# RWKV-7 recurrence on one Trainium2 core: the three sums over a head's channels as two fp32r products instead of one fp32 product

## The reference, cut to what matters

```
kk = heads(k * k_k)
kk = kk / jnp.maximum(jnp.linalg.norm(kk, axis=-1, keepdims=True), L2_EPS)
k = k.astype(f32) * (1.0 + (a - 1.0) * k_a.astype(f32))
...
y = wkv7_scan(rh, heads(decay), kh, vh, kk, kk * ah)
y = head_group_norm(y, lnx_w.astype(f32), lnx_b.astype(f32))
bonus = (jnp.sum(rh * kh * r_k.astype(f32), axis=-1, keepdims=True) * vh)
y = (y + bonus.reshape(bsz, t, D_INNER)) * jax.nn.silu(g.astype(f32))
```

## Time and profile before

| | |
|---|---|
| Runs of the kernel (3) | 2086.11, 2092.5, 2094.26 us; median 2092.5 |
| Span of the profiled execution | 2084.5 us |
| Its own time | not shown apart from the runs; the nearest, 2086.11 us, is 1.6 us above the span |
| Busy in the span | PE 1908.8 us (92%), DVE 1257.7 (60%), ACT 910.5 (44%), POOL 90.9 (4%) |
| `lerp_phase` | 0 to 237 us |
| `rwkv_phase` | 237 to 894 us |
| `dense_phase` | 894 to 2084.5 us |
| Period of a steady step | 37.5 us (POOL's `ld`, L619, starts at 591.87, 629.36, 667.29 us) |
| The three sums in all | L874, L869 and L879, 16 products each |

### The profile page before, as it was taken

The page is one execution under the profiler, slowest core; times in us unless marked ns, Lnnn a source line. Parts: engine busy times, 40 slices in busy tenths (PEclk is TensorE's granted clock), DMA queues, the critical chain, the costliest instruction groups (busy, mean ns, idle before and its releaser), DMA issues.

```text
span 2084.5 us, 43656 instructions
## 1 busy us (share of the span) xinstructions
PE 1908.8 (92%) x18912; PEld 1476.3 (71%) x18912; DVE 1257.7 (60%) x1865; ACT 910.5 (44%) x1392; POOL 90.9 (4%) x119
## 2 busy tenths in 40 slices
PE   4999799899999998989999999999888599999997
PEld 3678566666666666668888888887655378888885
DVE  6562167677777877644455554546557568777532
ACT  5342245646646556533222222335445464444321
POOL 2000000000000000300000000000011000000000
PEclk9999899999999999999999999999998799999998
DMA  3225311011111110143322223231110032222331
GB/s 121 77 80 151 99 44 41 29 45 41 34 40 41 44 40 30 53 132 103 101 97 96 101 91 101 91 101 61 51 41 21 15 107 92 101 97 95 94 91 68
DMA packets 51452, 154.13 MB, mean 74 GB/s; under 512 B 8512, under 2 KB 11072, under 8 KB 51264
## 3 DMA queue, kind: packets, MB, share of 16 engines
q1 hardware_dynamic: 51264, 151.35, 22.5%
HBM read 145.04 MB, written 6.29 MB: 73 GB/s over the span
## 4 chain that ended last, share of the span: by engine, by line
PE 50%; DVE 4%; ACT 2%; issue 1%; POOL 0%; DMA 0%; POOLq 0%; DVEq 0%; ACTq 0%
PE bank L1579 14%; PE bank L1578 14%; PE bank L1580 14%; PE bank L1666 1%; PE bank L1667 1%; PE bank L1668 1%; PE bank L1703 0%; DVE room L2288 0%; DVE room L2255 0%; PE bank L1686 0%; PE bank L1747 0%; PE bank L1738 0%; PE bank L1649 0%; PE bank L1714 0%; PE bank L1711 0%
## 5 line engine op out<-in xcount | busy, mean ns | idle before, releaser
L1785 ACT ACTIVATE w_hi<-raw 128x1024 fp32r<-128x1024 f32 (+2 forms) x195 | 197.7, 1015 | 496.3 <-PE bank L1580 453.9
L1578 PE MATMUL bank<-h_hi,w_hi 128*128 128x512 f32 x896 | 349.8, 390 | 0.0
L1580 PE MATMUL bank<-h_hi,w_lo 128*128 128x512 f32 x896 | 348.6, 389 | 0.0
L1579 PE MATMUL bank<-h_lo,w_hi 128*128 128x512 f32 x896 | 348.6, 389 | 0.0
L151 DVE TENSOR_TENSOR w_lo<-raw,w_hi 128x1024 fp32r<-128x1024 f32 (+2 forms) x202 | 237.0, 1174 | 153.6 <-ACT w_hi L1785 153.1
L1579 PEld LDWEIGHTS bank<-h_lo,w_hi 128*128 128x128 f32 x896 | 168.2, 188 | 35.7 <-issue 0.7
L1578 PEld LDWEIGHTS bank<-h_hi,w_hi 128*128 128x128 f32 x896 | 168.2, 188 | 35.3 <-issue 0.7
L1580 PEld LDWEIGHTS bank<-h_hi,w_lo 128*128 128x128 f32 x896 | 168.2, 188 | 35.0
L738 ACT ACTIVATE swapT<-invT 64x256 f32<-64x256 f32 x192 | 79.7, 415 | 104.4 <-DVE invT L1291 53.9
L144 PE MATMUL bank<-xg_hi,g_hi 128*128 128x512 f32 x256 | 104.0, 406 | 21.2 <-DVE g_lo L151 11.8
L145 PE MATMUL bank<-xg_lo,g_hi 128*128 128x512 f32 x256 | 102.1, 399 | 0.0
(11 more groups left out here) (377 smaller groups left out, 4126.8 us busy)
## 6 DMA issues: line engine op xcount, KB each, us to landing
raw<-in_w_conv SPq DMA_DIRECT2D x64, 512.0 KB, 3.2
raw<-in_w_up SPq DMA_DIRECT2D x44, 512.0 KB, 3.2
raw<-in_w_out SPq DMA_DIRECT2D x32, 512.0 KB, 3.8
raw<-in_w_in SPq DMA_DIRECT2D x20, 512.0 KB, 3.3
g_raw<-in_w_g SPq DMA_DIRECT2D x16, 512.0 KB, 3.3
g_raw<-in_w_r SPq DMA_DIRECT2D x16, 512.0 KB, 3.8
w_k<-in_w_k SPq DMA_DIRECT2D x16, 512.0 KB, 3.4
w_v<-in_w_v SPq DMA_DIRECT2D x16, 512.0 KB, 3.8
```

The costliest lines, as they stand in the source:

```text
L1578: pe.matmul(to, whi, hi, start=begin, stop=False)
L1579: pe.matmul(to, whi, lo, start=False, stop=False)
L1580: last = pe.matmul(to, wlo, hi, start=False, stop=end)
L1785: act.activation(w_hi[:, g % RING, 0:width], raw[:, g % RAW, 0:width], ACT.Copy).then_inc(S("whi"), 1)
```

## The change

Each of the three sums becomes two fp32r products, of the high and of the low part, added in the PSUM bank. POOL makes the parts: the high one by a multiplication by 1.0 that writes fp32r, the low one by a subtraction. The parts lie over tiles that are free at that time: `nn_hi` over `cum`, `yv_hi` over `rh`, `bon_hi` over `vT`, and each low part over its whole. The ones and the 1/64 are rounded in place to fp32r, by ACT, once. In POOL's `step` the making of the parts is put before, between and behind what stood there; in the last step the `y_lo` are made in two lots, ten before the parts of `yv` and five behind them.

```diff
+        halves = {"nsq": (nn, over_("nn_hi", cum_at, T), over_("nn_lo", nn_at, T)),
+                  "ysq": (yv, over_("yv_hi", rh_at, T), over_("yv_lo", yv_at, T)),
+                  "bon": (kraw, over_("bon_hi", vT_at, T), over_("bon_lo", kraw_at, T))}
...
         @block.gpsimd
         def _(pool):
+            def halved(sem, n):
+
+                whole, hi, lo = halves[sem]
+                pool.wait_ge(S(sem), n + 1)
+                apart(pool)
+                pool.tensor_scalar(hi[:, :], whole[:, :], 1.0, None, ALU.mult).then_inc(S(sem + "_hi"), 1)
+                pool.wait_ge(S(sem + "_hi"), n + 1)
+                apart(pool)
+                pool.tensor_tensor(lo[:, :], whole[:, :], hi[:, :].bitcast(F32), ALU.subtract)\
+                    .then_inc(S(sem + "_lo"), 1)
+
+            def key_halves(n):
+                need(pool, S("kd"), n)
+                need(pool, S("bet"), n)
+                halved("nsq", n)
+
+            def read_halves(n):
+                need(pool, S("bonus"), n)
+                need(pool, S("turn_mm"), 4 * (n - 1) + 2)
+                halved("bon", n)
...
             def step(c, p=None):
                 q = c % 2 if p is None else p
-                if not (isinstance(c, int) and c == IC - 1):
+                last = isinstance(c, int) and c == IC - 1
+                if not last:
+                    key_halves(c + 1)
                     prepare(c + 1, 1 - q)
+                if last:
+                    pool.wait_ge(S("inv0"), 2 * IC)
+                    out_halves(range(10))
+                if not (isinstance(c, int) and c == 0):
+                    halved("ysq", c - 1)
+                if not last:
+                    read_halves(c + 1)
                     chunk_ends(c + 1, 1 - q)
 
             pool.memset(decays[:, :, 0:1], 1.0).then_inc(S("ones"), 1)
+            key_halves(0)
             prepare(0, 0)
+            read_halves(0)
             chunk_ends(0, 0)
             run(step)(pool)
...
+            out_halves(range(10, IC - 1))
+            halved("ysq", IC - 1)
...
+            for n, exact in (("head_sum", head_sum), ("head_mean", head_mean)):
+                act.activation(exact[:, :], C[n], ACT.Copy).then_inc(S("exact"), 1)
...
+            def over_heads(sem, n, to, weights):
+
+                _, hi, lo = halves[sem]
+                pe.wait_ge(S("exact"), 2)
+                pe.wait_ge(S(sem + "_hi"), n + 1)
+                pe.matmul(to[:, :], weights[:, :], hi[:, :], start=True, stop=False)
+                pe.wait_ge(S(sem + "_lo"), n + 1)
+                return pe.matmul(to[:, :], weights[:, :], lo[:, :], start=False, stop=True)
+
             def variances(c):
-                pe.wait_ge(S("ysq"), c + 1)
-                pe.matmul(ROT[0][:, :], C["head_mean"], yv[:, :], start=True, stop=True).then_inc(S("var_mm"), 1)
+                over_heads("ysq", c, ROT[0], head_mean).then_inc(S("var_mm"), 1)
 
             def key_sums(n):
-                pe.wait_ge(S("nsq"), n + 1)
                 pe.wait_ge(S("tanh_a"), n + 1)
-                pe.matmul(GK[:, :], C["head_sum"], nn[:, :], start=True, stop=True).then_inc(S("nn_mm"), 1)
+                over_heads("nsq", n, GK, head_sum).then_inc(S("nn_mm"), 1)
 
             def bonus_sums(n):
                 pe.wait_ge(S("nclamp"), n + 1)
-                pe.wait_ge(S("bon"), n + 1)
-                pe.matmul(GK[:, :], C["head_sum"], bon[:, :], start=True, stop=True).then_inc(S("bsum_mm"), 1)
+                over_heads("bon", n, GK, head_sum).then_inc(S("bsum_mm"), 1)
```

More of the change, by code:

```diff
@@ L174, in program @@
         bank = [psum[:, i, :] for i in range(8)]
+        con_at = -(-nc.sbuf_base // 32) * 32
         con = sbt(top, "con", [P, NCON])
@@ L179, in program @@
         V = {n: par[:, PCOL[n]:PCOL[n] + k // P] for n, k in PARAMS}
-        K = dict(nc=nc, ins=ins, out=out, bank=bank, psum=psum, C=C, V=V, eps=eps, con=con, par=par, sbt=sbt, pair=pair)
+        K = dict(con_at=con_at, nc=nc, ins=ins, out=out, bank=bank, psum=psum, C=C, V=V, eps=eps, con=con, par=par, sbt=sbt, pair=pair)
         with ExitStack() as right:
@@ L526, in rwkv_phase, with placed @@
         lora = sbt(ctx, "w_lora2", [P, P])
-        kap, bet, kd, vT = (sbt(ctx, n, [P, T]) for n in ("kap", "bet", "kd", "vT"))
+        def placed(name):
+            at = -(-nc.sbuf_base // 32) * 32
+            return sbt(ctx, name, [P, T]), at
+        over_ = lambda name, at, cols: nc.alloc_sbuf_tensor_at(name, [P, cols], F32R, offset=at)
+        kap, bet, kd = (sbt(ctx, n, [P, T]) for n in ("kap", "bet", "kd"))
+        vT, vT_at = placed("vT")
         rt, bonus = sbt(ctx, "rt", [P, 2, T]), sbt(ctx, "bonus", [P, 2, T])
         ends = sbt(ctx, "ends", [P, 2, NCH])
-        ld, cum, tha, kp, kraw, kk, nn, rraw = (
-            sbt(ctx, n, [P, T]) for n in ("ld", "cum", "tha", "kp", "kraw", "kk", "nn", "rraw"))
+        ld = sbt(ctx, "ld", [P, T])
+        cum, cum_at = placed("cum")
+        tha, kp = (sbt(ctx, n, [P, T]) for n in ("tha", "kp"))
+        kraw, kraw_at = placed("kraw")
+        kk = sbt(ctx, "kk", [P, T])
+        nn, nn_at = placed("nn")
+        rraw = sbt(ctx, "rraw", [P, T])
         decays = sbt(ctx, "decays", [P, NCH, HD + 1])
@@ L549, in rwkv_phase @@
         swapT = sbt(ctx, "swapT", [P, TB, HD])
-        rh = sbt(ctx, "rh", [P, T])
+        rh, rh_at = placed("rh")
         phi = sbt(ctx, "phi", [P, NCH, HD])
         st = sbt(ctx, "st", [P, NCH, HD])
-        yc, yv = sbt(ctx, "yc", [P, T]), sbt(ctx, "yv", [P, T])
+        yc = sbt(ctx, "yc", [P, T])
+        yv, yv_at = placed("yv")
+        halves = {"nsq": (nn, over_("nn_hi", cum_at, T), over_("nn_lo", nn_at, T)),
+                  "ysq": (yv, over_("yv_hi", rh_at, T), over_("yv_lo", yv_at, T)),
+                  "bon": (kraw, over_("bon_hi", vT_at, T), over_("bon_lo", kraw_at, T))}
+        sums_at = K["con_at"] + 4 * CCOL["head_sum"]
+        head_sum, head_mean = (over_("exact_" + n, sums_at + 4 * P * k, P) for k, n in enumerate(("sum", "mean")))
+        K["head_mean"] = head_mean
         chan = sbt(ctx, "chan", [P, 2, 6])
@@ L615, in _, with out_halves @@
         def _(pool):
+            def halved(sem, n):
[15 more added lines that the diff above has]
+                halved("bon", n)
+            def out_halves(ks):
+                for k in ks:
+                    pool.wait_ge(D("y1_hi"), k + 1)
+                    pool.tensor_tensor(y[1][:, k, :], gate[:, k, :], y[0][:, k, :].bitcast(F32), ALU.subtract)\
+                        .then_inc(D("y1_lo"), 1)
             def prepare(n, p):
@@ L1754, in attention @@
                         pe.wait_ge(S("dsq"), n // 2 + 1)
-                        pe.matmul(bank[6][:, :], C["head_mean"], dsq, start=True, stop=True).then_inc(S("dv_mm"), 1)
+                        pe.matmul(bank[6][:, :], K["head_mean"][:, :].bitcast(F32), dsq, start=True, stop=True).then_inc(S("dv_mm"), 1)
                     fill(n, 9)
```

5 lines of the change are left out of this document (removed).

## The result

The changed kernel takes **2102.5 us** (median of 6 runs, 2099.3 to 2104.1) against 2093.3 of the kernel before, run beside it (6 runs, 2084.7 to 2096.6). The recorded ratio, which isn't the quotient of the two medians (1.0044), is 1.0056, with 1.0039 to 1.0073 as its 95% interval: slower by about 0.5%, where 2089.0 was forecast and 2082 to 2097 was the range. The time missed the range by 5.5 us and the sign of the effect was wrong.

The account below looks back on a forecast made before the run. The PE was taken to bound a steady step at `bonus_sums`, up to the DVE's 1.05 us of idling. -5.9 + 0.5 + 0.5 + 1.5 = -3.4 us, applied to the median of 2092.5, gave 2089 us, range 2082 to 2097.

Parts of the forecast that it names:

- POOL's high part: POOL in each step: the scaling takes 0.62 us, a pair of parts 2.06 us, with 0.16 before it.
- An idle PE before L930 would mean that POOL is late, which I exclude.: Sign in a steady step: POOL's parts come in time, so the PE has no new wait before L930.
- The price of a sum: Each sum: f32 product 1.12 us, two fp32r products 0.73, gain 0.39 us, between nothing and 0.6.
- the places where it counts: Steady steps: only `bonus_sums` gains, 15 x 0.39 = -5.9 us; `key_sums` and `variances` give nothing.
- the steady period: Steady steps of the recurrence: the period falls from 37.5 us to near 37.1.
- the estimate of 0.53 us by the number of passes: Each sum: FP32 takes four passes, reduced FP32 one, so half of 1.06 us is gained; steady steps give 8.0 us.
- The DVE beside POOL: Steady step: `kk` waits for POOL's low part of `bon`, 0.55 us late, still hidden; costed at nothing.
- The cover of 1.05 us: Steady step: the DVE's idle time before the states, which hides its delays; 0.1 us was to be left.
- slower, by the DVE: Rival, steady steps: `kk` and `tha` take 1.1 us more each, a step 1.15 us longer, 2112 us; chance 0.05.
- Before the first step: Start of the recurrence: the PE waits for POOL's parts, +0.5 us, between -0.6 and +2.2.
- The last step and behind it: Late `y_lo` stall the PE, +0.5 us (-0.4 to +1.2); pair 15's logarithm starts later, +1.5 us (0 to +2.5).
- the edges eat it: Rival: steady steps give 0 to -2 us, edges cost +2.5 to +5, time 2093 to 2097; chance 0.2.

Follow-up runs that it names:

- e1: The changed kernel with POOL's high parts made by two operations (times 1.0, plus 0.0) in place of one: 2094.3 us, ratio 1.0014.
- e7: The changed kernel with only `bonus_sums` of pairs 1 to 15 in parts, high parts by two operations, all other sums in f32: ratio 0.9994.
- e2: The changed kernel with the variances back in one f32 product, no POOL parts of `yv`, high parts still one operation: 2095.0 us, ratio 1.0015.
- e8: The kernel before with seven additional POOL operations on 128x384 in five steps, to time their forms; its one run's time says nothing.
- e6: The changed kernel, high parts by two operations, f32 products for pair 0's `nn`, `bon` and variances 14, 15, `y_lo` in one lot: 2084.5 us, ratio 0.9983.

## Why the prediction was wrong

- **POOL's high part: the term that failed.** "A scaling of 128x512 takes 0.62 us" was taken from the earlier trace rows, the nearest in size, engine and name. Those rows are scalings with two operations; the change's has one. It takes 1.49 on the same engine and tile, and 0.62 again in e1, which adds the second operation and changes nothing else. The pair is 1.49 + 0.15 + 1.27 = 2.9 us and not 2.06. The forecast gave this price no upper bound, although the diff shows the second operation left out and no row of before has that form.
- **"An idle PE before L930 would mean that POOL is late, which I exclude."** It was: the PE was idle there in each of 13 steps, for 0.86 us in nine of them and 0.48 to 0.78 in the other four. The reason given for excluding it rested on the 0.62. The working also dealt with `nn`, `yv` and `bon` one after the other, while POOL's queue carries the lateness of `nn_hi` on to `yv_lo`; at 0.62 us a part that made no difference. And a part that is up to 1 us late was to be hidden before `NTG`: the wait there is only some 0.57 us in e1, and `yv_lo` was 1.02 us late.
- **The price of a sum, the places where it counts, the steady period:** right. 0.73 us for the pair, nothing for `key_sums` and `variances` (e7), 37.08 for "near 37.1" (e1). The period fell by 0.40 us, so the price from the rows held, and the estimate of 0.53 us by the number of passes was too high. With the slow form the period is 37.66 instead, and the step's gain of 0.40 us is a loss of 0.18.
- **The DVE beside POOL:** the mechanism was right. Four times, in the fences or the same steps, a DVE operation began while POOL was subtracting: the scan of the changed kernel 0.63 us before `yv_lo` ended, `kk` of e1 0.92, `tha` of e2 1.11 and the small copy 1.24 us before `bon_lo` ended. They took 0.50, 0.78, 0.97 and 1.10 us longer than alone, each time what was left of the subtraction less 0.13 or 0.14. From 262 to 842 us of all the runs, 184 operations of the DVE (165 that read two SBUF tiles, and 19 times the small copy) began more than 0.2 us before the end of a subtraction, and every one grew by what was left less 0.13 to 0.15 us. That isn't a slower pace but a wait until the other is through. 213 operations that read a PSUM bank began there too, and none grew.

  The 0.78 of `kk` is from a step that other idle time disturbs. In the common step of e1 it is 0.49 (1.18 against 0.69), where 0.55 was forecast:

```profile
679.21 1.18 DVE L1248 TENSOR_TENSOR kk<-kk,nn 128x512 f32<-128x512 f32 x1 [1.68 <-ACT nn L766]
...
684.69 0.28 DVE L1305 TENSOR_SCALAR st<-bank,ends 128x64 f32<-128x64 f32 x1 [0.19 <-PE bank L1187]
```

  The cover of 1.05 us holds: less the 0.40 by which the states come earlier and the 0.49 of `kk` it leaves 0.16, against the 0.19 shown. In the changed kernel `bon_lo` is 0.87 us later and hits `tha` or the copy. The rival "slower, by the DVE" had this mechanism, but wanted two full hits (2.2 us on the queue, 1.15 us a step) and gave 2112 us; what came is a step longer by 0.18 us, and by the PE's wait.

  The section "Who interferes with whom" of the page SBUF — State Buffer of the Trainium skill says that VectorE and GpSimd share a port pair as an exclusive lock: a VectorE instruction with two SBUF inputs, or a copy or scaling in a 2-port mode, blocks until GpSimd's is over. The rows agree where POOL subtracts, the copy of two columns among them. They don't where POOL makes a high part, which reads SBUF too: in the changed kernel all of the fifteen `kk` that began beside `bon_hi` took 0.69 us as alone, up to 0.97 us before its end. In e8 `kd`, beside one of the seven forms, took 0.98 us in place of 0.69, so a one-input operation isn't always free either. There the measurements decide; what sets these cases apart isn't shown.
- **Before the first step:** +0.5 forecast, between -0.6 and +2.2; measured +3.6 to +3.9 with the slow form and +0.3 to +0.6 in e1. Part of the former is the clock, which the forecast had in its upper bound: from 265 to 268 us it was 0.50 in the changed kernel, 0.81 before and 0.78 in e1. **The last step and behind it:** +0.5 and +1.5 forecast, together +1.6 with the -0.4 of `bonus_sums(15)`, which lies in the same stretch; measured +2.7 with the slow form and +2.0 in e1 (+2.9 against e6, which has the f32 product at the edges). The first term was right for the part's assumed time, the two last together somewhat low; they weren't measured apart. Behind the last step 0.6 to 0.7 of the 0.87 us of a high part shows.
- **The sum.** With 0.62 us, that is e1, the terms give the period and nearly both edges, but the forecast left out the idle time without a releaser and the stretches at half clock: +6.0 and +1.5 us in e1's 14 steps against before, more than the gain of 5.6. -3.4 us was forecast; e1's recurrence is +1.9 to +3.6 us. Its 2094.3 us lies in the 2093 to 2097 of the rival "the edges eat it", but not by that rival's mechanism, since its common step gains the full 0.40 us. The range took 4 us from the scatter of the runs of one kernel; the scatter between builds is its own term.

## What to carry to other kernels

Price an added operation from a row of the same form, operand for operand: on POOL here a multiplication by 1.0 costs 1.49 us with one operation and 0.62 with a second, idle one, on the same tile. On an engine that gets several new jobs in a row, add their lateness along its queue before you compare it with each reader's cover. And if a change is to gain 0.4 us in a step, use it only in the steps where a wait shows that it pays: here one of the three sums gave all of the gain, and the uncovered sums at both ends cost 3.4 us (e1 against e6), as much as eight steps brought.
